# Norms and head outputs handed on by halves, gate rows made in stages of their own, a block's last slot on TensorE, and activation tables asked for ahead

## What is computed

```python
h = rmsnorm(x, norm_attn_g[l]) * (1 + sc1) + sh1
y, yc = parallel_mixers(h, hc, p, ang_mla, ang_diff, lam, lam_init, not last)
x = x + g1 * y
h = rmsnorm(x, norm_ffn_g[l]) * (1 + sc2) + sh2
x = x + g2 * peer_ffn(h, p)
```

## Time and profile before

| | |
|---|---|
| median of 3 runs | 2643.49 us |
| the profiled execution's own time | 2648.58 us |
| its span | 2645.9 us |
| PE, DVE, ACT, POOL busy | 78%, 70%, 43%, 37% |
| moved by DMA | 980.26 MB, 370 GB/s over the span |
| of it the gathers' queue | 855.69 MB |

### The profile page before, as it was taken

The page is one execution under the profiler, slowest core; times in us unless marked ns, Lnnn a source line. Parts: engine busy times, 40 slices in busy tenths (PEclk is TensorE's granted clock), DMA queues, the critical chain, the costliest instruction groups (busy, mean ns, idle before and its releaser), DMA issues.

```text
span 2645.9 us, 26377 instructions
## 1 busy us (share of the span) xinstructions
PE 2068.0 (78%) x6888; PEld 1083.2 (41%) x6888; DVE 1854.0 (70%) x4486; ACT 1149.7 (43%) x3047; POOL 975.7 (37%) x916
## 2 busy tenths in 40 slices
PE   5997787876978877888777697879777887677766
PEld 2455443543444445444334244334543444333322
DVE  0146986895557878885979765654597786867776
ACT  2123494344236644753433723432245654433332
POOL 1012333332434333543343444420133443445553
PEclk8998888888989988989889998989888988888988
DMA  8587999997999999999999999996599999999997
GB/s 338 159 298 293 387 385 387 396 395 299 382 389 391 363 409 390 382 383 411 412 409 390 402 415 405 398 405 234 184 412 388 415 351 394 415 382 420 422 421 308
DMA packets 215418, 980.26 MB, mean 370 GB/s; under 512 B 17628, under 2 KB 75512, under 8 KB 116984
## 3 DMA queue, kind: packets, MB, share of 16 engines
q0 software_dynamic: 123648, 855.69, 79.6%
q1 hardware_dynamic: 91640, 123.05, 13.6%
HBM read 977.62 MB, written 1.05 MB: 370 GB/s over the span
## 4 chain that ended last, share of the span: by engine, by line
PE 32%; DVE 25%; DMA 21%; ACT 12%; issue 8%; POOL 1%; SPq 0%; POOLq 0%; DVEq 0%; ACTq 0%
DMA EXPERT<-in_peer_uv,FIX 20%; PE VS L985 12%; PE PA L844 9%; DVE EXPERT L1595 8%; DVE ACC L1605 3%; DVE SCR L1221 2%; PE PA L872 2%; PE PB L773 1%; PE PB L975 1%; ACT L1169 1%; ACT WEI L1171 1%; PE VS L802 1%; PE PB L912 1%; POOL EXPERT L681 1%; ACT DIAG L1176 1%
## 5 line engine op out<-in xcount | busy, mean ns | idle before, releaser
L985 PE MATMUL VS<-EXPERT,DIAG 128*128 128x512 f32 x2304 | 1174.9, 651 | 253.9 <-ACT DIAG L1176 251.7
L681 POOL DMA_INDIRECT EXPERT<-in_peer_uv,FIX x768 | 901.2, 1173 | 1083.5 <-PE VS L985 704.4
L1595 DVE CUSTOM_DVE_ANT_0 EXPERT<-EXPERT,H 128x1024 f32<-128x1024 f32 x768 | 925.0, 1224 | 327.7 <-DMA EXPERT<-in_peer_uv,FIX 318.2
L985 PEld LDWEIGHTS VS<-EXPERT,DIAG 128*128 128x128 f32 x2304 | 458.0, 210 | 829.0 <-issue 480.0
L1169 ACT ACTIVATE GEL<-DOT 128x1 f32<-128x1 f32 x768 | 155.0, 202 | 1028.1 <-DVE DOT L1595 1013.8
L844 PE MATMUL PA<-WT,HT 128*128 128x512 f32 (+2 forms) x720 | 298.6, 560 | 20.3 <-ACT KTD L1099 7.4
L1605 DVE SCALAR_TENSOR_TENSOR ACC<-EXPERT,WEI,ACC 128x1024 f32<-128x1024 f32 x192 | 245.9, 1281 | 25.9 <-ACT WEI L1171 24.0
L1176 ACT ACTIVATE DIAG<-IDN,WEI 128x128 f32<-128x128 f32 x576 | 231.3, 402 | 62.9 <-PE VS L985 44.5
L975 PE MATMUL PB<-HT,WT 128*128 128x128 f32 (+1 forms) x1472 | 212.7, 305 | 39.9 <-issue 36.3
L1171 ACT ACTIVATE WEI<-GEL,GATE 128x1 f32<-128x1 f32 x768 | 226.3, 295 | 24.9
L975 PEld LDWEIGHTS PB<-HT,WT 128*128 128x128 f32 x1472 | 205.4, 216 | 64.8 <-issue 58.7
(11 more groups left out here) (146 smaller groups left out, 1730.0 us busy)
## 6 DMA issues: line engine op xcount, KB each, us to landing
EXPERT<-in_w_ada POOLq DMA_DIRECT2D x48, 1024.0 KB, 11.3
WT<-in_peer_wq SPq DMA_DIRECT2D x92, 512.0 KB
WT<-in_w_in SPq DMA_DIRECT2D x48, 512.0 KB
WT<-in_w_out SPq DMA_DIRECT2D x48, 512.0 KB
EXPERT<-in_peer_uv,FIX POOLq DMA_INDIRECT x768
WT<-in_w_in SPq DMA_DIRECT2D x16, 384.0 KB
WT<-in_w_in SPq DMA_DIRECT2D x16, 288.0 KB
WT<-in_mla_wq_up SPq DMA_DIRECT2D x4, 512.0 KB
```

What stands on the lines that cost most here:

```text
L681: pool.indirect_dma_start(out=EXPERT[:, j, :], out_offset=None, in_=a["peer_uv"], in_offset=bass.IndirectOffsetOnAxis(ap=FIX[:, par, j:j + ...
L985: ins = nc.tensor.matmul(VSUM[n][:, :], DIAG[:, i, :], EXPERT[:, j, D + n * W:D + (n + 1) * W], start=first, stop=last_one)
L1595: nc.vector.tensor_tensor_reduce(out=EXPERT[:, j, 0:D], in0=EXPERT[:, j, 0:D], in1=H2[:, b % HB, :], scale=1.0, scalar=0.0, op0=ALU.mult, ...
```

## The change

Norms: the square, the scaling and the wait of TensorE are by halves of 512 columns, and `x_ready` counts halves. Products and the first key query wait for the half of HT that they read. `gate_rows` for g1 is in two `rows` stages, ahead of and behind `heads`; in two of the attentions the diagonals for it (`gates`) stand earlier. `close` is split. `foot`, ahead of slot 125, multiplies what ACC has by the gate, adds it onto X and leaves the gate row in ACC; the rest, slot 127 on TensorE too (LASTD), is multiplied and added in the new `close`. A one-element activation asks for the table of Sqrt ahead of two norms and for Exp ahead of two attentions. The final scaling and the output go by halves. The diff below has first the plan and the tiles, then TensorE, ScalarE and VectorE.

```diff
+FOOT = SLOTS - BY_PE
...
-    return out + [("gates", l, g, t), ("hnorm", l, g, t), ("heads", l, g, t)]
+    return out + [("gates", l, g, t), ("hnorm", l, g, t), ("rows", l, g, t, 0), ("heads", l, g, t), ("rows", l, g, t, 1)]
+
+def gates_early(stages, after):
+    gates = next(s for s in stages if s[0] == "gates")
+    rest = [s for s in stages if s != gates]
+    return rest[:after] + [gates] + rest[after:]
...
-        while at < to and picked(stream[at]) and not (stream[at][0] == "close" and (holds(s) or keeps_gates(s) or splits_pick(s))):
+        while at < to and picked(stream[at]) and not (stream[at][0] == "foot" and (holds(s) or keeps_gates(s) or splits_pick(s))):
...
 def stream_of(b, first=0, last=SLOTS):
-    return [("slots", b, i, i + 1) for i in range(first, last)] + ([("close", b)] if last == SLOTS else [])
+    out = []
+    for i in range(first, last):
+        out += ([("foot", b)] if i == FOOT else []) + [("slots", b, i, i + 1)]
+    return out + ([("close", b)] if last == SLOTS else [])
...
-    attend, leave, first = attention(0, CTX, 0), outward(0, CTX, (0,)), pick_apart(0, CTX)[0]
+    attend, leave, first = gates_early(attention(0, CTX, 0), 4), outward(0, CTX, (0,)), pick_apart(0, CTX)[0]
...
-    keys, attend, leave = front(1, LAT, (1,), queries=False), attention(1, LAT, 0), outward(1, LAT, (0,))
+    plan.insert(plan.index(("foot", 3)) + 1, ("wide", 1))
+    keys, attend, leave = front(1, LAT, (1,), queries=False), gates_early(attention(1, LAT, 0), MH + 3), outward(1, LAT, (0,))
...
-        GROW = SCR[:, D + 2 * W:D + 3 * W]
+        GROW = SCR[:, 2048:3072].rearrange("p (n c) -> p n c", n=2)
...
             def norm(stage):
-                pe.wait_ge(xn_ready, tick("norm"))
                 for half in range(2):
+                    pe.wait_ge(xn_ready, tick("norm"))
                     bank = fill_b()
...
-                held["ht", stage[3]] = rb.n
+                    held["ht", stage[3], half] = rb.n
+
+            def half_there(ts, half):
+                for t in ts:
+                    pe.wait_ge(emptied_b, held["ht", t, half])
...
                 if part == 0:
-                    if kind == "out":
-                        gate_rows()
-                    pe.wait_ge(emptied_b, rb.n)
                     held["banks"] = [fill_a() for t in ts]
                     held["fills"] = ra.n
+                if part % (PARTS // 2) == 0:
+                    half_there(ts, part // (PARTS // 2))
...
+            def rows(stage):
+                gate_rows()
...
                 for k in range(KD):
+                    if first and k % (KD // 2) == 0:
+                        half_there(ts, k // (KD // 2))
...
+                    elif v0 == SLOTS - 1:
+                        pe.wait_ge(last_diag, b + 1)
+                        for n in range(2):
+                            nc.tensor.matmul(VSUM[n][:, :], LASTD[:, :], EXPERT[:, RING - 1, D + n * W:D + (n + 1) * W],
+                                             start=False, stop=True).then_inc(last_used, 1)
-            def close(stage):
+            def foot(stage):
                 for n in range(2):
                     gate_rows()
...
+            def mean_square(tile, place, changes):
+                for half in range(2):
+                    at = slice(half * W, (half + 1) * W)
+                    if changes:
+                        act.wait_ge(x_ready[tile], 2 * changes - 1 + half)
+                    link(nc.scalar.activation(place[:, at], X[:, tile, at], ACT.Square, accum_out=NS[:, half:half + 1]))
+                    if half == 0:
+                        nc.scalar.activation(NE[:, :], NS[:, 0:1], ACT.Identity, scale=1.0 / D, bias=EPST[:, :])
+                nc.scalar.activation(NQ[:, :], NS[:, 1:2], ACT.Sqrt, scale=1.0 / D, bias=NE[:, :]).then_inc(root_ready, 1)
...
+                if (l, tile, which) == (1, 3, 1):
+                    table_of(ACT.Sqrt)
...
-                nc.scalar.activation(XN[:, t % 2, :], X[:, tile, :], ACT.Copy, scale=NR[:, :]).then_inc(xn_ready, 1)
+                for half in range(2):
+                    at = slice(half * W, (half + 1) * W)
+                    nc.scalar.activation(XN[:, t % 2, at], X[:, tile, at], ACT.Copy, scale=NR[:, :]).then_inc(xn_ready, 1)
+
+            def table_of(function):
+                nc.scalar.activation(IDLE[:, :], EPST[:, :], function)
...
+                if h == 0 and t == 0 and l == g:
+                    table_of(ACT.Exp)
...
+                        if v0 == SLOTS - 1:
+                            act.wait_ge(wei_ready, slot_no(b, v0) + 1)
+                            if b > 0:
+                                act.wait_ge(last_used, 2 * b)
+                            nc.scalar.activation(LASTD[:, :], IDN[:, :], ACT.Copy, scale=WEI[:, BY_PE:BY_PE + 1])\
+                                .then_inc(last_diag, 1)
...
             def last_(stage):
                 t = stage[1]
-                act.wait_ge(x_ready[2 + t], 4)
+                if t == 1:
+                    table_of(ACT.Sqrt)
...
+            def rows(stage):
+                _, l, g, t, n = stage
+                bank = from_a()
+                if n == 0:
+                    diagonals(l, g, 1, 1)
+                nc.vector.tensor_copy(GROW[:, n, :], bank[:, :]).then_inc(emptied_a, 1)
+                dve.wait_ge(emptied_a, ra.n)
...
-            def close(stage):
+            def foot(stage):
                 b = stage[1]
                 l, tile = block_home(b)
-                no = slot_no(b + 1, 0)
                 diagonals(l, tile // 2, 2, 0)
-                apply(no - 1, (b + 1) * QUADS - 1, RING - 1)
-                rows = [from_a()]
+                bank = from_a()
                 diagonals(l, tile // 2, 2, 1)
-                dve.wait_ge(used_dve, (b + 1) * QUADS)
-                dve.wait_ge(used_pe, (b + 1) * QUADS * BY_PE)
...
+                dve.wait_ge(used_dve, (b + 1) * QUADS - 1)
+                for n, half in enumerate(HALVES):
+                    if n == 1:
+                        bank = from_a()
+                    link(tt(ACC[:, half], ACC[:, half], bank[:, :], ALU.mult))
+                    x = X[:, tile, half]
+                    link(tt(x, x, ACC[:, half], ALU.add))
+                    nc.vector.tensor_copy(ACC[:, half], bank[:, :]).then_inc(emptied_a, 1)
+                dve.wait_ge(emptied_a, ra.n)
+
+            def close(stage):
+                b = stage[1]
+                l, tile = block_home(b)
+                for n, half in enumerate(HALVES):
+                    dve.wait_ge(last_used, 2 * b + n + 1)
+                    if n == 1:
+                        dve.sem_inc(used_dve, 1)
+                    tt(ACC[:, half], VSUM[n][:, :], ACC[:, half], ALU.mult).then_inc(vsum_read, 1)
+                    dve.wait_ge(vsum_read, 2 * b + n + 1)
+                    x = X[:, tile, half]
+                    tt(x, x, ACC[:, half], ALU.add).then_inc(x_ready[tile], 1)
+                dve.wait_ge(x_ready[tile], 4 * l + 4)
```

More of the change, by code:

```diff
@@ L158, in keeps_gates @@
 def keeps_gates(s):
-    return s[0] in ("gates", "hnorm", "heads") or (s[0] == "out" and s[3] == 0)
+    return s[0] in ("gates", "hnorm", "heads") or (s[0] == "rows" and s[4] == 0)
 def products(l, n):
@@ L199 @@
 COST = {"stat": (45, 0), "norm": (50, 0), "in": (0, 20), "turn": (0, 10), "root": (5, 5), "up": (0, 25), "attn": (35, 0),
-        "hnorm": (20, 0), "heads": (20, 0), "gates": (10, 0), "out": (0, 22), "back": (20, 0), "pick": (45, 0), "more": (40, 0), "also": (45, 0), "then": (40, 0),
+        "hnorm": (20, 0), "heads": (20, 0), "gates": (10, 0), "rows": (10, 0), "out": (0, 22), "back": (20, 0), "pick": (45, 0), "more": (40, 0), "also": (45, 0), "then": (40, 0),
         "ada": (18, 0), "adae": (4, 0), "adat": (10, 0), "mod": (5, 0)}
@@ L384, in landings @@
     return sum(home(i) == home(m) for i in range(m + 1))
-FINAL_GAIN_AFTER = sum(s[0] == "norm" for s in PLAN[:PLAN.index(("norm", DEPTH - 1, CTX, 1, 1)) + 1])
+FINAL_GAIN_AFTER = 2 * sum(s[0] == "norm" for s in PLAN[:PLAN.index(("norm", DEPTH - 1, CTX, 1, 1)) + 1])
 def parts_of(i0, i1):
@@ L1009, in _ @@
             do = {"consts": consts, "tables": tables, "ada": ada, "adat": adat, "norm": norm, "back": back, "in": product, "out": product,
-                  "up": up, "turn": turn, "attn": attn, "heads": heads, "pick": pick_, "more": more, "slots": slots,
-                  "close": close}
+                  "up": up, "turn": turn, "attn": attn, "heads": heads, "rows": rows, "pick": pick_, "more": more, "slots": slots,
+                  "foot": foot}
             for stage in PLAN:
@@ L1655, in last_ @@
                 dve.wait_ge(fg_in, 16)
[L1656 to L1658 removed]
+                for half in HALVES:
+                    x = X[:, 2 + t, half]
+                    nc.vector.scalar_tensor_tensor(out=x, in0=x, scalar=NR[:, :], in1=X[:, 0, half], op0=ALU.mult,
+                                                   op1=ALU.mult).then_inc(y_ready, 1)
```

(2 more changed lines are left out.)

84 lines of the change are left out of this document (30 added, 54 removed).

## The result

The kernel after takes 2671.78 us (median of 6 runs, 2662.55 to 2673.98), before 2647.71 in the same comparison: a ratio of 1.0086, interval 1.0065 to 1.0106. It is slower, and the time lies above the prediction's range; rival 2, with 2662, is the nearest. The profiled execution took 2670.99 us with a span of 2669.0 (before 2645.9).

What follows compares the result with a forecast made beforehand. DMA was taken to bound the gathers, a TensorE, VectorE and ScalarE chain the stretches before, between the layers and after. 6.0 + 0.1 - 5.5 + 3.5 = +4.1 gave 2647.6, called 2648 us, no change that can be told; range 2631 to 2664.

Steps and rivals of the forecast that it cites:

- rival 2: At every block's end: foot's wait delays hand-back of slots 125 to 127, DMA never recovers; +5 each, 2662, chance 0.31.
- While gathers run: Gather stages: split stalls at four block ends +6, fewer TensorE waits -2.5; together +3.5 (-10 to +20).
- +1.5 each: +6: Four block ends: DMA runs dry 2 or 3 us per block where it did not; bounds 0 to +8 each.
- what 8 buffers hold ahead of it is some 11 slots, 27 us: Block ends: transfers issued ahead cover VectorE's stall, 22.6 us after against 14.3 before, plus 7 for slow slot and issue.
- DVE's extra work, 1.6 a block, lies beside DMA: Gather stages: VectorE's added 1.6 us a block runs beside DMA transfers and adds nothing to the sum.
- The end of the last block: Last block's tail: foot and slow TensorE delay close, +8.3; half squares, early table load and output gain 2.3; +6.0.
- Between the layers: Fourth block's end to next gathers: first product +4.2, later steps -4.1; stage +0.1.
- Before the first gather: Start of kernel: fewer HT and copy waits, earlier Exp table, row sums, second norm; -5.5 (-8 to -3).
- Rivals 3 and 4: ScalarE tables: 3, replaced again before use, +3, 2651, chance 0.05; 4, switches hold longer, -5, 2643, chance 0.02.
- rival 4's figure: ScalarE table switches: 1.3 us more for each of four loads moved off a path, -5, 2643; chance 0.02.
- The stage list: Gather stages: the list is interleaved by costs that the new rows stages shift; no sign given.
- DMA shares below 0.37 and 0.55: Stages behind block ends: lower shares than these would speak for rival 2, higher ones for shorter, hidden stalls.

Runs made afterwards that it cites:

- e9: e1 plus three linked VectorE operations (3.75 us) right behind close, at the ends of blocks 0, 1, 2 and 4; 2641.60 us, ratio 0.9978.
- e5: Kernel after with foot behind slot 127, ahead of close, and slot 127's buffer freed by TensorE's last matmul; 2663.00 us, ratio 1.0070.
- e6: Kernel after, foot staying ahead of slot 125, with slot 127's buffer freed by TensorE's last matmul; 2671.05 us, ratio 1.0102.
- e12: e3 with the last slot's buffer freed by TensorE's last matmul; 2639.12 us, ratio 0.9966.
- e1: Kernel after with the block's end alone put back: no foot, slot 127 on VectorE, one close behind it; 2631.28 us, ratio 0.9933.
- e3: Kernel after without foot, slot 127 staying on TensorE, all gate work behind dot 127; 2635.20 us, ratio 0.9949.
- e11: Kernel after with foot moved behind slot 127 and joined with close in one stage; 2649.16 us, ratio 1.0006.
- e16: Kernel after with 16 products of a zero matrix on TensorE behind foot's row sums, to keep it at work; 2662.98 us, ratio 1.0063.
- e15: e1 with close's first gate diagonals ahead of dot 126 and their row sums right behind TensorE's slot 125; 2640.04 us, ratio 0.9974.
- e10: e1 plus three linked VectorE operations ahead of slot 66, mid-block, in blocks 0, 1, 2 and 4; 2641.71 us, ratio 0.9970.
- e7: e1 with TensorE's products and first key query waiting for all banks of the B ring again; 2646.37 us, ratio 1.0007.
- e14: e1 without the one-element activations that ask for tables ahead; 2634.60 us, ratio 0.9945.
- e2: Kernel before with foot, the new close and slot 127 on TensorE alone; 2698.79 us, ratio 1.0176.
- e13: e1 without the rows stages, gate rows and diagonals made where they were before the change; 2628.69 us, ratio 0.9933.

## Why the prediction was wrong

- **The step that failed** is the term for the four block ends in "While gathers run": "+1.5 each: +6". The ends grew by 25.2 us, and nothing of it was made up. The sum held a reserve, "what 8 buffers hold ahead of it is some 11 slots, 27 us", against a stretch of 14.3 us before and 22.6 after, with 7 more for the reissue: 21 us before, inside the reserve, and 30 after, 2 or 3 beyond it. The difference was near (8.3 worked out; 6.3, 7.4, 4.6 and 6.9 measured), but both lengths were far too short: the ends were 38.5, 26.9, 20.2 and 23.0 us, and the reissue came 27.6 to 46.5 us behind dot 124. VectorE also works on the picks there (before the change, at block 1's end, some 8 us between 1030.16 and 1040.57). So the reserve was used up before the change, or all but used up (block 2), and the 6 us of slack that would have taken in most of the stall were not there. The earlier trace rows showed it, with shares of 0.37 and 0.55; they were cited and left out of the +1.5. Where transfers already stand still, a further us is lost nearly whole: e9 puts a known stall there and finds 0.7 to 0.8 us of total for a us.
- **Rival 2** had the right sign and place, at +5 for an end, and said that DMA never makes the stall up. Its mechanism, the late hand-back of the buffers of slots 125 to 127, is not borne out. In after the gathers into them came up to 39.0, 40.7 and 42.5 us behind dot 124 (block 0; before 14.8, 19.9 and 31.7), and yet at all four ends no one of the next block's dots 1 to 7 waited for DMA (the longest idle ahead of one is 0.03 us). They took 9.2, 12.8, 17.7 and 14.3 us from dot 0 to dot 7, before 9.2, 17.7, 17.7 and 14.4. The next transfers behind those eight start with the ninth gather, which waits for the use of slot 0; late buffers among the eight only shift when the transfers stand still. What counts is how long VectorE takes from dot 124 to the next dot 0. Handing slot 127's buffer back sooner gained nothing either (e5, e6, e12).
- The price of foot over e1, 40 us, is by steps: last slot on TensorE 4 (e3), foot's added work on VectorE 15 (e11), and 21 for its place ahead of slot 125 (after against e11), in which TensorE's lower clock has some 6 to 9 (e16). The single steps are each uncertain by some 5 us or more. In the profiles after is longer than e11 by 2.2, 8.2, 0.4 and 3.2 at the four ends: most of it is at block 1, where in after a pick's stages stand between dot 127 and close, with a wait of 3.17 us of VectorE for TensorE in them. At block 0 dots 125 to 127 stand with foot behind an output product, as in e15; that end is some 8 longer than e1's.
- **"DVE's extra work, 1.6 a block, lies beside DMA"** was wrong too: foot's added work is 15 us in five ends and the last (e11 against e3), and even in the middle of a block a us of VectorE is not free (e10).
- **The end of the last block:** +4.9 for +6.0. Foot ran from 2643.68 to 2651.35 with its first multiplication behind TensorE's slot 124, the dots stood in a row, slots 125 and 126 took 6.46 us. Close ended 22.4 us behind dot 124 instead of 15.4: +7.0, predicted +8.3. TensorE was fast ahead of foot here, which the earlier trace rows did not have. Gains behind close: 2.1, predicted 2.3, with the table load gone from ahead of the root. One reading was wrong, without weight in the sum: DMA waits stand ahead of dots 126 and 127 only; dot 125 (2625.55) follows the accumulation directly.
- **Between the layers:** -0.9 for +0.1, right by its steps and not only in sum. The first product is 4.0 later against dot 124 (1792.08 less 1762.43, before 25.7), predicted +4.2; from there to dot 0 it is 4.8 shorter, predicted 4.1. TensorE's four adaLN pieces stood where they were expected, from 1784.91:

```profile
1784.91 3.64 PE L820 MATMUL VS<-EXPERT 128*32 128x512 f32 x32
1789.03 1.27 PE L791 MATMUL PB<-IDN,SCR 128*128 128x128 f32 x8 [0.48 <-ACT SCR L1104]
1790.22 1.92 PE L820 MATMUL VS<-EXPERT 128*32 128x512 f32 x16
1792.08 7.13 PE L867 MATMUL PA<-WT,HT 128*128 128x512 f32 x16
```

- **Before the first gather:** -11.2 for -5.5, of which some 2 is luck. The waits were priced at their length, 1.4 and 1.4 and a part of the second norm. Together they are 8.3 in the profiles of e7 and e1. At the key query it is 3.9, of which 2.4 are slow passes at a granted clock of 0.50; a further 1.5 are 24 passes of an adaLN product, 4.30 us from 115.21 in e7 and 2.78 from 111.92 in e1. The first product, 46.98 before, now starts at 43.34: 3.6 earlier, of which the first HT write was already 2.5 earlier.
- **Rivals 3 and 4** are out by the rows: no table came back, since the load at 2655.89 is followed by a root without one, and before and after have 240 loads each. The loads asked for ahead are together worth about 3 within some 7 (e14), so the times alone tell their rows' 3.5 neither from nothing nor from rival 4's figure. The Trainium skill (ScalarE: Activation LUTs, "What ACT_TABLE_LOAD costs") has some 1283 ns of load and some 1380 ns of drain for a switch. The load agrees, 1.28 us in all 240; the drain does not show on either side of one: in the median a load starts 0.02 us behind the instruction ahead of it, and the next starts 0.01 us behind the load. The measurement decides.
- **The stage list:** the sign left open is a loss in block 4's inner time. It is 370.0 to 370.7 us in the three kernels without the rows stages (before, e2, e13) and 373 to 382 in the fifteen with them.
- **The total:** the sum is 19 us off in the profiles: +19.2 at the four ends and +7.6 in the inner time, less 5.7, 1.0 and 1.1 in the other rows. Without what came out better ahead of the first gather it would have been further off.

That DMA shares below 0.37 and 0.55 behind the ends would speak for rival 2 was a usable sign for the loss, and over 40 us the shares tell it plainly, 0.89 to 0.71 and 0.91 to 0.73. It does not tell late buffers from a late dot 0; the waits ahead of the next block's dots do.

## What to carry to other kernels

A ring of buffers is no reserve where it has already run out: ask of a stretch whether its transfers stand still now, and if they do, price each added us at nearly a us, whatever the mean rate is. Measure the stretch in the trace; the sum here counted only the operations at hand, 14.3 us, where 20 to 38 went by. What a split adds on the engine that must start the next block is paid at every block, while what it brings forward may be wanted only at the last one. Price a wait of TensorE with what its clock does behind it.

## What the runs showed of the hardware

TensorE's granted clock can fall behind pauses of 2 to 5 us. Behind 5.20 us two slots took 6.32 us at 0.58; with products of zeros in the pause, 3.70 at 1.00. Behind 1.94 us of waiting 18 passes took 4.18 us at 0.50, where behind 0.44 and 0.17 they went at 0.12 to 0.14 each at 1.00. The stages behind these pauses:

```profile
2309.17:2315.49 6.32, 6.32 (x9) 2.74 (x10) 1.24 (x4) 1.80 (x6) 0.94 (x1) 0.58 0.45 178
2301.62:2305.32 3.70, 3.70 (x9) 1.79 (x10) 1.24 (x4) 1.80 (x6) 0.91 (x1) 1.00 0.92 383
208.00:212.30 4.30, 4.25 (x20) 4.28 (x21) 0.00 (x0) 0.27 (x1) 0.00 (x0) 0.50 0.02 6
```

The length of the pause alone does not decide: an idle of the same 2.26 us stood ahead of the same transposes in e7 and in e1, and the 24 adaLN passes behind them took 4.30 us at 0.64 in e7 and 2.78 at 1.00 in e1. At the key query the price, 3.9 us, was 2.6 times the later start of 1.5, so shortening or filling such a pause can pay more than its length.
